# Attention layers of a four-layer trunk: projections in halves, eight units placed among them, one output tile ahead of the rest

## The reference

```
swa:  q, k, v = h @ w_qkv          # 16 query heads, 4 key/value heads of 64
      q, k = axial_rope(q), axial_rope(k)
      context: softmax(q k^T / 8, with a sink logit per head) v
      latent:  the same over 128 own and 128 cached keys
na:   q, k, v = h @ w_qkv          # 16 heads of each, no rope
      latent:  adds a position bias to the 128 own keys
both: out = heads(o) @ w_o ;  new k, v of the context are outputs
```

## Time and profile before

| | |
|---|---|
| median of 3 runs | 2099.66 us |
| the profiled execution | 2096.02 us, its span 2094.2 us |
| PE busy | 93% of the span |
| DVE, ACT, POOL busy | 60%, 45%, 11% |
| DMA | 413 MB, 197 GB/s on average |
| TensorE's mean granted clock | 0.966 of full |
| layer 1, projections to the end of the output projection | 687.2 to 830.6 us |
| layer 2, the same | 1051.7 to 1239.8 us |

### The profile page before, as it was taken

How to read it: one execution, slowest core, us unless ns; L and a number is a source line. 1 busy time by engine, 2 the same in 40 slices (tenths; PEclk the granted TensorE clock), 3 DMA queues, 4 the chain that set the end, 5 groups by cost and what they waited for, 6 DMA issues and landing times.

```text
span 2094.2 us, 32644 instructions
## 1 busy us (share of the span) xinstructions
PE 1938.3 (93%) x13994; PEld 1723.5 (82%) x13994; DVE 1264.8 (60%) x1749; ACT 942.2 (45%) x1385; POOL 221.0 (11%) x171
## 2 busy tenths in 40 slices
PE   5999999999999868999987689999999999989998
PEld 2899775898999646999975379998899776889998
DVE  2744675557875534787444357865844665657864
ACT  2643345435553333555333336553643345535552
POOL 1100110002110110111000101110100110001110
PEclk7999999999999988999998789999999999999999
DMA  7554347757554644655564456456544447644551
GB/s 315 188 213 164 141 161 299 264 186 272 205 197 177 226 157 170 248 220 183 192 268 144 158 204 235 187 198 223 216 168 161 159 161 265 220 161 161 182 183 60
DMA packets 65824, 413.01 MB, mean 197 GB/s; under 512 B 11744, under 2 KB 12048, under 8 KB 17424
## 3 DMA queue, kind: packets, MB, share of 16 engines
q1 hardware_dynamic: 53856, 392.19, 50.7%
q10 hardware_dynamic: 11824, 18.74, 2.6%
HBM read 400.10 MB, written 10.76 MB: 196 GB/s over the span
## 4 chain that ended last, share of the span: by engine, by line
PE 79%; issue 7%; DVE 6%; ACT 4%; POOL 2%; DMA 1%; SPq 0%; POOLq 0%; DVEq 0%; ACTq 0%
PE ps L519 13%; PE ps L498 13%; PE ps L499 13%; PE ps L500 13%; PE ps L537 5%; PE ps L539 5%; PE ps L538 5%; PE ps L876 2%; PE ps L550 2%; DMA raw<-in_stream 1%; PE ps L764 1%; ACT Ea L1175 1%; PE ps L748 1%; PE ps L581 1%; POOL hf L1777 1%
## 5 line engine op out<-in xcount | busy, mean ns | idle before, releaser
L423 DVE TENSOR_TENSOR spl_lo<-raw,spl_hi 128x1024 fp32r<-128x1024 f32 x556 | 710.3, 1308 | 326.2 <-ACT spl_hi L412 325.3
L412 ACT ACTIVATE spl_hi<-raw 128x1024 fp32r<-128x1024 f32 x556 | 567.9, 1054 | 371.3 <-PE ps L539 195.1
L498 PE MATMUL ps<-H_hi,spl_hi 128*128 128x256 f32 x1920 | 550.2, 287 | 18.8 <-DVE H_lo L1338 17.9
L499 PE MATMUL ps<-H_lo,spl_hi 128*128 128x256 f32 x1920 | 546.5, 285 | 0.0
L500 PE MATMUL ps<-H_hi,spl_lo 128*128 128x256 f32 x1920 | 546.3, 285 | 0.0
L498 PEld LDWEIGHTS ps<-H_hi,spl_hi 128*128 128x128 f32 x1920 | 371.6, 194 | 37.7 <-issue 37.7
L499 PEld LDWEIGHTS ps<-H_lo,spl_hi 128*128 128x128 f32 x1920 | 371.8, 194 | 0.0
L500 PEld LDWEIGHTS ps<-H_hi,spl_lo 128*128 128x128 f32 x1920 | 371.7, 194 | 0.0
L537 PE MATMUL ps<-G_hi,spl_hi 128*128 128x256 f32 x704 | 200.3, 284 | 5.9 <-DVE spl_lo L423 5.9
L538 PE MATMUL ps<-G_lo,spl_hi 128*128 128x256 f32 x704 | 199.2, 283 | 0.0
L539 PE MATMUL ps<-G_hi,spl_lo 128*128 128x256 f32 x704 | 199.2, 283 | 0.0
(11 more groups left out here) (232 smaller groups left out, 2860.1 us busy)
## 6 DMA issues: line engine op xcount, KB each, us to landing
raw<-in_stream SPq DMA_DIRECT2D x374, 1024.0 KB, 4.8
out_new_C<-c_stage ACTq DMA_DIRECT2D x16, 512.0 KB, 5.6
ada_b<-in_ada_b ACTq DMA_DIRECT2D x4, 768.0 KB, 8.4
x<-in_x ACTq DMA_DIRECT2D x1, 1024.0 KB, 12.1
cache<-in_na_cache ACTq DMA_DIRECT2D x1, 1024.0 KB, 9.0
bias<-in_rpb ACTq DMA_DIRECT2D x1, 1024.0 KB, 13.6
small<-in_small ACTq DMA_DIRECT2D x1, 838.5 KB, 7.6
cache<-in_swa_cache ACTq DMA_DIRECT2D x1, 512.0 KB, 6.9
```

The lines of the kernel that those rows point to most:

```text
L412: act.activation(spl_hi[m % SPL][:, :], raw[r % RAW][:, h * HALF:(h + 1) * HALF], ACT.Copy).then_inc(S["hi_done"], 1)
L423: dve.tensor_tensor(spl_lo[m % SPL][:, :], raw[r % RAW][:, h * HALF:(h + 1) * HALF], spl_hi[m % SPL][:, :].bitcast(F32), ALU.subtract).the ...
L498: pe.matmul(out, w_hi, x_hi, start=st, stop=False, skip_group_check=True)
L499: pe.matmul(out, w_hi, x_lo, start=False, stop=False, skip_group_check=True)
```

## The change

- The projections work on halves of 512 output columns. A tile now holds 4 k-blocks x 512 columns, `half_rows` is 12 matmuls for each half tile as before. swa: kv into banks ACC0 and ACC1 ("A"), q's first half into UP1 and the MISC bank ("B"), its second half into A. na: first halves of q (A), k (B), v (A), then the second halves of q, k, v, all in A. A half needs only its own eighth of the activations (`h_done`), not the whole norm.
- As soon as the first halves stand, heads 0 to 7 (units 0 to 3) can run. In na they are placed among the second halves of q, k, v; in swa q's last tile stands between scores(0) and scores(1). Units 4 to 7 come after the transposes of the second halves.
- Three units are in flight: in the steady part PE's order is scores(u+1), ada tiles, transposes(u), values(u-1). There is now one pair of score banks, so `scores` waits for the exponentials of the unit before. `PTa` has two buffers; the upper half of a wide unit's `PTa` is copied by DVE, as is the middle bank of the keys.
- The results of the units go to `O_hi` and `O_lo`, so that H stays whole for the second halves.
- The first output tile `o0` now holds k-blocks 0 to 3 of pair 0 (first half) and pair 1 (second half), so it needs units 0 to 3 alone. It is fetched and split early, and its two halves are multiplied between the last units. Pairs 0 and 1 end together after the second tile, then pairs 2 and 3.
- rope works on pieces of 512 columns, the first of them between splits.
- The order of the stream follows; the number of tiles and matmuls is the same.

```diff
+                halves = [("q", i, h, t) for h in range(2) for t in range(2)]
+                stage([("kv", i, t) for t in range(2)] + halves, 2 * i)
+                fill(1)
+                order.append(o[0])
+                fill(7)
+                order.append(o[1])
+                fill(3)
...
+            def half_rows(tile, banks, h_base=None):
+                t = tile[-1]
+                for h in range(2):
+                    m = 2 * INDEX[tile] + h
+                    pe.wait_ge(S["lo_done"], m + 1)
+                    if h_base is not None:
+                        pe.wait_ge(S["h_done"], h_base + 2 * t + h + 1)
+                    for k in range(2):
+                        for s in range(NS):
+                            a_hi, a_lo = both(H_hi, H_lo)(4 * t + 2 * h + k, s)
+                            for a, w in ((a_hi, spl_hi), (a_hi, spl_lo), (a_lo, spl_hi)):
+                                mm = pe.matmul(banks[s][:, :], a, w[m % SPL][:, k * 512:(k + 1) * 512],
...
                 def scores(u):
-                    if w >= 2:
-                        pe.wait_ge(S["exp_done"], 4 * w - 4)
+                    if w:
+                        pe.wait_ge(S["exp_done"], 4 * w)
```

PE's order in swa, after the first halves and their keys (waits left out as "..."):

```diff
+                    queries(0, (ACC[2], ACC[3]), 1, 2)
+                    fill(1)
...
+                    scores(0)
+                    half_rows(("q", i, 1, 1), A)
+                    scores(1)
+                    fill(2)
+                    weights(0)
+                    scores(2)
+                    mod_rows(i, 1)
+                    weights(1)
+                    values(0)
+                    scores(3)
+                    queries(1, A, 2, 3)
+                    weights(2)
+                    values(1)
...
+                    scores(4)
+                    fill(1)
+                    weights(3)
+                    values(2)
+                    scores(5)
+                    fill(2)
+                    weights(4)
+                    values(3)
+                    scores(6)
+                    fill(2)
+                    weights(5)
+                    values(4)
+                    scores(7)
+                    output_half(0)
+                    weights(6)
+                    values(5)
+                    output_half(1)
+                    weights(7)
+                    values(6)
+                    fill(2)
+                    values(7)
+                    fill(1)
```

PE's order in na, after scores(0) and an ada tile, up to the last units:

```diff
+                    half_rows(("qkv", i, 0, 1, 0), A)
+                    scores(1)
+                    weights(0)
+                    half_rows(("qkv", i, 0, 1, 1), A)
+                    scores(2)
+                    weights(1)
+                    values(0)
...
+                    half_rows(("qkv", i, 1, 1, 0), A)
+                    scores(3)
+                    weights(2)
+                    values(1)
+                    half_rows(("qkv", i, 1, 1, 1), A)
+                    weights(3)
+                    values(2)
+                    fill(1)
...
+                    half_rows(("qkv", i, 2, 1, 0), A)
...
+                    queries(1, (ACC[2], ACC[3]), 7)
+                    values(3)
+                    half_rows(("qkv", i, 2, 1, 1), A)
...
+                    keys(1)
+                    fill(1)
...
+                    scores(4)
...
+                    output_half(0)
+                    mod_rows(i, 1)
+                    scores(5)
+                    output_half(1)
+                    weights(4)
```

DVE's order in na around units 1 and 2 (ACT splits the same tile between the exponentials of units 1 and 2), then its steady order in swa:

```diff
+                    maxima(1)
+                    split("qkv", i, 1, 1, 0)
+                    reciprocals(1)
+                    used("qkv", i, 0, 1, 1)
+                    rows(qrow, 1, ACC[1])
+                    maxima(2)
+                    reciprocals(2)
+                    weights(1)
+                    attended(0)
+                    split("qkv", i, 1, 1, 1)
```

```diff
+                    reciprocals(3)
+                    attended(1)
+                    maxima(4)
+                    reciprocals(4)
+                    weights(3)
+                    attended(2)
+                    maxima(5)
```

More of the change, by code:

```diff
@@ L138, in chunked, with unit, pair_end @@
     return w[k0 * P:(k0 + nk) * P, c0:c0 + nc].reshape(nk, P, nc).transpose(1, 0, 2).reshape(P, nk * nc)
+def unit(u, nk):
+    if nk == KD and u < 4 * nk:
+        half, rest = divmod(u, 2 * nk)
+        pair, rest = divmod(rest, nk)
+        return pair, half * nk // 2 + rest // 2, rest % 2
+    pair, rest = divmod(u, 2 * nk)
+    return pair, rest // 2, rest % 2
+def pair_end(pair, nk):
+    return 1 + max(u for u in range(8 * nk) if unit(u, nk)[0] == pair)
 def units(w, t):
-    nk = w.shape[0] // P
     out = []
     for u in range(16 * t, 16 * t + 16):
-        pair, rest = divmod(u, 2 * nk)
-        k, o = rest // 2, 2 * pair + rest % 2
+        pair, k, rest = unit(u, w.shape[0] // P)
+        o = 2 * pair + rest
         out.append(w[k * P:(k + 1) * P, o * P:(o + 1) * P])
@@ L501, in weights_stationary, with rows_stationary @@
                     mm.then_inc(S["half_used"], 1)
-            def rows_stationary(n, chunk, first, last, width=1024, banks=None):
+            def rows_stationary(n, chunk, first, last):
                 for h in range(2):
@@ L507, in rows_stationary @@
                     pe.wait_ge(S["lo_done"], m + 1)
-                    per = HALF // width
-                    for k in range(per):
-                        for s in range(NS):
[L511 to L520, removed]
+                    for s in range(NS):
+                        a_hi, a_lo = chunk(h, s)
+                        for a, parts in ((a_hi, (spl_hi, spl_lo)), (a_lo, (spl_hi,))):
+                            for w in parts:
+                                for c in range(2):
+                                    st = first and h == 0 and a is a_hi and w is spl_hi
+                                    en = last and h == 1 and a is a_lo
+                                    mm = pe.matmul(ACC[2 * s + c][:, :], a, w[m % SPL][:, c * 512:(c + 1) * 512], start=st,
+                                                   stop=en, skip_group_check=True)
@@ L784, in attention @@
                 nb = 4 if a == 0 else 8
[L785 to L803, removed]
@@ new lines, in keys @@
+                def keys(hh):
+                    for b, bank in enumerate((ACC[2], ACC[3], UP[0])):
+                        for p in range(4):
+                            blk, src = divmod(12 * hh + 4 * b + p, 3)
+                            rows = cache[:, blk * P:(blk + 1) * P] if src == 2 else \
+                                krow[:, src * nb * P + blk * P:src * nb * P + (blk + 1) * P]
+                            mm = pe.transpose(bank[:, p * T:(p + 1) * T], rows, ident)
+                        mm.then_inc(S["tk_mm"], 1)
@@ new lines, in used, with rows, queries, keys @@
+                def used(*tile):
+                    tile_used(act, INDEX[tile])
+                def rows(t, hh, bank):
+                    copy(t[:, hh * 512:(hh + 1) * 512], bank[:, :], "row_a")
+                def queries(hh, bank):
+                    act.wait_ge(S["tq_mm"], 4 * a + 2 * hh + 1)
+                    copy(qT[:, 2 * hh * 512:(2 * hh + 1) * 512], bank[:, :], "tq_a")
+                def keys(hh):
+                    for b, bank in ((0, ACC[2]), (2, UP[0])):
+                        act.wait_ge(S["tk_mm"], 3 * (a + hh) + b + 1)
+                        copy(kT[:, (3 * hh + b) * 512:(3 * hh + b + 1) * 512], bank[:, :], "tk_a")
@@ L1196, in ffn @@
+                split("o", i, 1)
+                weights(7)
+                attended(6)
+                attended(7)
+                project(INDEX["o", i, 0], 4, KD, 2 * i + 1, 1)
             def ffn(i):
@@ L1577, in head_columns, with rope @@
                 ins.then_inc(S["hc_done"], 1)
[L1579 to L1584 removed]
+            def rope(t, c0, count):
+                if count:
+                    dve.wait_ge(S["roped"], count)
+                heads, w = 8, 512
                 xv, uv = (ap.rearrange("p (h f e w) -> p h f e w", f=2, e=2, w=16)
@@ L1629, in attention, with split, used, rows @@
-                for b in range(4):
-                    dve.wait_ge(S["tq_mm"], 4 * a + b + 1)
-                    dve.tensor_copy(qT[:, b * 512:(b + 1) * 512], ACC[b][:, :]).then_inc(S["tq_evac"], 1)
+                def split(*tile):
+                    split_lo(dve, INDEX[tile])
+                def used(*tile):
+                    tile_used(dve, INDEX[tile])
+                def rows(t, hh, bank):
+                    dve.tensor_copy(t[:, D + hh * 512:D + (hh + 1) * 512], bank[:, :]).then_inc(S["row_d"], 1)
@@ L1660, in maxima, with reciprocals @@
                                           ALU.mult).then_inc(S["nm_done"], 1)
-                maxima(0)
-                for u in range(8):
-                    g, s = u // 2, u % 2
+                def reciprocals(u):
                     w = 8 * a + u
-                    width = (1 + s) * T
```

528 lines of the change are left out of this document (361 added, 167 removed).

## The result

The changed kernel takes 2007.8 us (median of four, 2006.95 to 2009.0) against 2099.0 (median of four as well, one run more than stood before the prediction): a ratio of 0.957, 95% interval 0.955 to 0.958, 91 us less. Its profiled execution has a span of 2005.3 us, 88.9 less than before. The forecast was 2023 us and a range of 2000 to 2050.

What follows compares the result with a forecast made beforehand. A chain of units, no single engine, was taken as the bound. Layer 1 from 147.4 to 114.2 us and layer 2 from 192.1 to 150.6 save 75: 2021, plus half of 3.7 gives 2023 us; range 2000 to 2050.

Steps and rivals of the forecast that it cites:

- Floor: PE's own work in the new order at full clock: 98.6 us for layer 1, 132.7 for layer 2.
- counted waits: PE's remaining stalls, counted by following the engines' programs side by side: 8.8 us in layer 1, 10.1 in layer 2.
- the 13 us for clock, hops and port: Both layers, losses the wait count leaves out: 6 us for clock, 4 for hops between engines, 3 for the port.
- Clock: PE's clock drops after stalls in the two layers: three drops, 6 us; bounds 0 and 21 us.
- Port: DVE's `nm` held while POOL's instruction runs: three holes in each layer, half of each covered, 3 us.
- Hops: Passing work between engines in the two layers: 4 us.
- The start: Before each layer's first projection: idle time falls from 4.01 to 0.8 us, and the clock stays full.
- The other signs: First projection within 1 us of ada; one 3 to 6 us layer 2 wait; others under 2.5; clock 0.93 or more.
- a rival for the time: Nine splits among POOL's steps, each held up to 1.89 us: 17 us more, 2040 us; chance 0.06.
- Slow pace: In-order queues hold units at 8 us in 11 rounds without a projection: 27 us come back, 2050 us; chance 0.14.
- the slower rival: Nine splits queued behind unit steps on ACT and DVE starve PE, 12.2 us each: 110 us, 2133 us; chance 0.03.
- the rival near the floor: Engines' steps dodge each other, stalls halve and the 13 us shrink to 4: 2005 us; chance 0.08.

Runs made afterwards that it cites:

- the swap: Changed kernel with, on DVE in layer 2, unit 1's reciprocal sum before the split of the first tile of K's second half: 2005.4 us, ratio 0.956.
- the one with the rows first: Changed kernel with unit 1's sum and DVE's second query-row copy before that layer 2 split, and ACT's layer 1 query copy before unit 3's exponentials: 2003.1 us.

## Why the prediction was right, and where it was off

- **What bounds.** A chain, not an engine, in the units: right. With the chain overlapped, the idle time of two layers fell from 75 to 17 us with every other stretch as it was, and one unit less in flight brings back the waits for `PTa` and 34 us. But I named only those waits, 33.7 us; another 17.9 us before the transposes and 7.4 us before the output tile were there as well, and they are 7.6 and 1.6 us now.
- **Floor and waits.** Floor, start and counted waits without the 13 us for clock, hops and port come to 108.2 and 143.6 us, from the end of the third ada tile; measured were 106.9 and 144.5. Single waits came within 1 us: in layer 1, the 1.9, 1.7 and 1.0 us of the forecast were 1.13, 0.76 and 0.53; in layer 2's last units, its 0.6, 0.4, 1.6, 1.7 and 0.8 were 0.59, 0.47, 1.82, 1.19 and 0.79. (Unit 4's round, 4.9 less 3.8, is 1.1 and not 1.2.) The wait at unit 1's transposes was forecast at 4.4 us, for the split between maxima and sum; it was 4.29, and the swap that should remove it cut it to 0.60. In layer 1 PE's waits add up to 6.3 us instead of 9.6, and the clock took what was saved. So it is in part luck that the count without clock fits layer 1 to 1.3 us: two errors of about 3 us cancel.
- **The mis-sized term** is the 13 us for what such a count leaves out. Clock: I took three drops, 6 us; by their mean clock of 0.97 and 0.99 the two stretches lose 3.2 and 1.4 us, and the second profile of the same kernel, with layer 1 at 1.00, is only 1.9 us shorter there. Port: no split of the changed kernel stands beside a scaling of POOL, and each pair keeps its 2.36 us; what is longer beside one is `nm`, three times, 0.70, 0.72 and 0.58 us instead of 0.17. Hops: PE's measured waits contain them, and are no longer than the count (17.1 us with the start, against 20.5). So neither port nor hops showed as a loss of its own, and of the 13 us no more than 5 did, all clock. The forecast was 15 us high: 13 from this term, about 1 from the half of the distance to the median that I added (1.9, where 0.7 was found), the rest from stretches outside the two layers.
- **The start.** 0.8 us of idle forecast, 0.89 measured, full clock as forecast. Undoing it costs 7.3 us against the 8 to 9.5 worked out later.
- **A sign that missed.** Layer 1's attention, from the first projection to the last output tile, took 106.0 us (683.99 to 789.95) and not 107 to 118; layer 2's 143.6 lies at the lower edge of 143 to 156. The other signs came as stated.
- **The port.** Where a split of DVE does stand beside POOL it is held: two halves took 2.94 us in the run with the sum first and 2.76 in the one with the rows first, instead of 2.36. The Trainium skill ("SBUF — State Buffer", "SBUF: two separate sides") states such a hold for DVE instructions with two SBUF inputs, and this trace agrees. As a rival for the time it was far too dear, at nine splits and 1.89 us each: in the changed kernel none was held.
- **The rivals.** Slow pace (8 us a unit) did not come: the rounds of layer 1 from scores(4) to scores(7) take 4.6, 5.6 and 4.7 us. PE waited 0.28 and 0.7 us for a split in all, so the slower rival, 8.3 us a split, was not near. By its mechanism the result is the forecast's, waits much as counted; by its time, 2007.8, it lies just under the forecast's own range (2008 to 2040) and beside the rival near the floor (2005). That rival had 0.08 and deserved more: the 13 us did shrink as it says, to 5 or less, though the stalls did not halve.

## What to carry to other kernels

Where one engine idles in a chain of short steps over several engines, follow the in-order programs side by side with durations from the trace, and add up the waits: it found each large wait here, to within 1 us. Add on top for small losses only what is not already inside a counted wait: here 13 us were added, and no more than 5 showed. A change of depth must be made in the order of every engine at once: PE alone at the wrong depth cost 20 us more than the whole pipeline at that depth. A wait list is to be read to its end: 25 us of waits that I had not named stood beside the ones that I had, and 16 of them went. And a split or copy that stands between two short steps of a chain is worth looking for: a reciprocal of 0.17 us behind a split was the longest wait left.

## What the runs showed of the hardware

- The same kernel with the same waits of PE (1.13, 0.53, some 0.7 us within 4 us) ran 10 us at a mean granted clock of 0.66 in one profile, 0.83 in another and 1.00 in a third; between the first and the last layer 1 differs by 1.9 us.
- Waits of 3.92 and 4.29 us were each followed by a few microseconds at half clock (1.71 and 1.97 us for eight transposes that take 1.09).
- A pair of DVE subtractions with both inputs in SBUF took 2.94 and, in another order, 2.76 instead of 2.36 us beside a multiplication on POOL.
